# Turning the merged chunks by VectorE and GpSimd DMAs, and adding x by accumulating DMAs, in a hybrid attention and RG-LRU layer

## The reference, cut to what matters

```
g = sigmoid(h @ w_gate + b_gate)          # two halves, g_a and g_r
merged = g_a * (y_a @ w_br_attn) + g_r * (y_r @ w_br_rnn)
out = merged @ w_out                      # 4096 x 4096
y = x + gate_res * out                    # gate_res: one value per channel
```

## Time and profile before

| | |
|---|---|
| median of 3 runs | 2569.64 us (2569.23 to 2569.82) |
| the profiled execution's own time | 2569.65 us |
| its span, first to last instruction | 2567.8 us |
| TensorE busy | 2534.8 us, 99% |
| VectorE busy | 2010.9 us, 78% |
| ScalarE busy | 1441.0 us, 56% |
| GpSimd busy | 38.2 us, 1% |

### The profile page before, as it was taken

One profiled execution on the slowest core, in us unless ns is written; L12 is line 12 of the kernel. 1 busy time (PEld: TensorE's weight loads), 2 busy tenths in 40 slices (PEclk: granted clock), 3 DMA queues, 4 the chain that ended last, 5 costly groups with the idle time before them and its releaser, 6 DMA issues.

```text
span 2567.8 us, 31417 instructions
## 1 busy us (share of the span) xinstructions
PE 2534.8 (99%) x11463; PEld 2102.1 (82%) x11463; DVE 2010.9 (78%) x2138; ACT 1441.0 (56%) x1712; POOL 38.2 (1%) x58
## 2 busy tenths in 40 slices
PE   6999999999999999999999999999999999999999
PEld 5888888888888888888888888888888888878887
DVE  6999999999887666675766766668787878778885
ACT  6787766655554465655666666543434444544453
POOL 0000000000000000220000000000000000000000
PEclk9999999999999999999999999999999999999999
DMA  9999999999998566556666666689898989666674
GB/s 351 360 329 348 349 366 356 378 366 353 354 359 288 171 195 187 156 162 196 194 198 199 194 200 198 201 320 352 306 356 311 351 312 349 212 219 214 205 238 164
DMA packets 374846, 700.86 MB, mean 273 GB/s; under 512 B 28082, under 2 KB 83620, under 8 KB 374436
## 3 DMA queue, kind: packets, MB, share of 16 engines
q1 hardware_dynamic: 374176, 698.72, 80.9%
q10 hardware_dynamic: 516, 0.13, 0.0%
HBM read 694.55 MB, written 4.21 MB: 272 GB/s over the span
## 4 chain that ended last, share of the span: by engine, by line
PE 97%; DVE 1%; ACT 1%; SPq 0%; issue 0%; DMA 0%; DVEq 0%; ACTq 0%
PE ps_acc L1629 27%; PE ps_acc L1564 25%; PE ps_acc L1566 25%; PE ps_t L1564 3%; PE ps_t L1566 3%; PE ps_t L1629 3%; PE ps_acc L1580 2%; PE ps_acc L1582 2%; PE ps_acc L1621 0%; PE ps_acc L1622 0%; PE ps_acc L1623 0%; DVE w_lo L996 0%; PE ps_t L1704 0%; SPq L606 0%; DMA ada_first<-in_w_ada 0%
## 5 line engine op out<-in xcount | busy, mean ns | idle before, releaser
L741 ACT ACTIVATE w_hi<-land 128x1024 fp32r<-128x1024 f32 x860 | 910.3, 1060 | 948.3 <-PE ps_acc L1566 614.1
L996 DVE TENSOR_TENSOR w_lo<-land,w_hi 128x1024 fp32r<-128x1024 f32 x860 | 1049.2, 1222 | 416.1 <-ACT w_hi L741 412.9
L1564 PE MATMUL ps_acc<-w_hi,h_hi 128*128 128x512 f32 x2324 | 907.3, 390 | 0.1
L1566 PE MATMUL ps_acc<-w_hi,h_lo 128*128 128x512 f32 x2324 | 904.5, 389 | 0.0
L1629 PE MATMUL ps_acc<-w_lo,h_hi 128*128 128x512 f32 x2564 | 685.7, 389 | 0.6 <-DVE w_lo L996 0.6
L1629 PEld LDWEIGHTS ps_acc<-w_lo,h_hi 128*128 128x128 f32 x2564 | 481.1, 188 | 101.4 <-DVE w_lo L996 1.4
L1564 PEld LDWEIGHTS ps_acc<-w_hi,h_hi 128*128 128x128 f32 x2324 | 436.3, 188 | 91.1 <-ACT ps_acc L880 0.5
L1566 PEld LDWEIGHTS ps_acc<-w_hi,h_lo 128*128 128x128 f32 x2324 | 436.4, 188 | 89.4
L1005 DVE SCALAR_TENSOR_TENSOR acc<-ada_ring,cvec,acc 128x1024 f32<-128x1024 f32 (+1 forms) x291 | 300.1, 1031 | 15.0 <-DMA ada_ring<-in_w_ada 8.3
L1406 DVE SCALAR_TENSOR_TENSOR racc<-res_land,cvec,racc 128x1024 f32<-128x1024 f32 x124 | 158.5, 1279 | 0.8 <-DMA res_land<-in_w_ada 0.7
L1564 PE MATMUL ps_t<-w_hi,h_hi 128*128 128x512 f32 x356 | 138.7, 389 | 0.0
(11 more groups left out here) (307 smaller groups left out, 2192.0 us busy)
## 6 DMA issues: line engine op xcount, KB each, us to landing
land<-in_w_in SPq DMA_DIRECT2D x384, 512.0 KB, 5.5
land<-in_w_gate SPq DMA_DIRECT2D x256, 512.0 KB, 4.5
ada_ring<-in_w_ada SPq DMA_DIRECT2D x160, 512.0 KB, 6.1
res_land<-in_w_ada SPq DMA_DIRECT2D x128, 512.0 KB, 7.7
land<-in_w_out SPq DMA_DIRECT2D x92, 512.0 KB, 4.4
ada_ring<-in_w_ada SPq DMA_DIRECT2D x140, 256.0 KB, 5.0
land<-in_w_br_attn SPq DMA_DIRECT2D x64, 512.0 KB, 4.3
land<-in_w_br_rnn SPq DMA_DIRECT2D x64, 512.0 KB, 5.8
```

Source lines behind the costliest of these rows:

```text
L741: act.activation(w_hi[:, n % PARTS], land[:, n % LAND], ACT.Copy).then_inc(hi_rdy, 1)
L996: dve.tensor_tensor(w_lo[:, n % PARTS], land[:, n % LAND], w_hi[:, n % PARTS].bitcast(F32), ALU.subtract).then_inc(split_done, 1)
L1564: pe.matmul(sums[:, t], l_hi(kk, t), w_hi[:, n % PARTS, kk], start=first and kk == 0 and not added, stop=False, skip_group_check=added)
L1566: ins = pe.matmul(sums[:, t], l_lo(kk, t), w_hi[:, n % PARTS, kk], start=False, stop=False, skip_group_check=added)
```

## The change

Three parts go together.

1. *Turning.* After the merged add of chunk k, VectorE turns the chunk in blocks of 32 by 32 by two transposes of 128 by 512 into `gate_turned`, which has the place of `gate`. GpSimd then issues sixteen DMAs, each of 32 partitions by 1 KB (32 KB), that put the blocks in place in `chunk_t[k]`. SP's bias load of the next block waits for these sixteen (`mt_in`) where it waited for `gate_used`. ScalarE and VectorE read `chunk_t` where they read `ps_t`; TensorE's transposes and the copies into `comb` are gone.
2. *x.* At units 600 and 624 SP issues two copies of x into y, DRAM to DRAM, each of 128 rows by 3584 columns (1.84 MB). The results of the first seven chunks are added to y by accumulating DMAs on GpSimd's queue. The loads of x and stores of y in SP's program go, but for the last chunk's.
3. *Emptying.* ScalarE copies LEFT and RIGHT (and "out" 0) into the SBUF tile `plain`, on which TensorE now waits (`plain_kept`), and VectorE joins from `plain`.

The diff, without the declarations of semaphores and some removed lines:

```diff
+X_AT = [N_R + 24, N_R + 48]
...
-    if FREED[j][0] == "dve" or JOBS[j][:2] == ("out", 0):
+    if FREED[j][0] == "dve":
...
+def by_block(tiles):
+    return tiles.rearrange("p k t (i b) -> p (k t) i b", b=32)
+def by_tile(blocks):
+    return blocks.rearrange("p i k t b -> p (k t) i b")
...
-        x_out = at("x_out", [P, 2, NT, CW], F32, blk(88))
+        plain = at("plain", [P, 4, CW], F32, blk(88))
...
-        comb = [at(f"comb{i}", [P, UK, NT, P], F32, blk(32 + 4 * i)) for i in range(SEVENS)]
+        gate_turned = at("gate_turned", [P, BPJ, BPJ, NT, 32], F32, r_scr)
+        chunk_t = [at(f"chunk_t{k}", [P, BPJ, BPJ, NT, 32], F32, blk(V_BLK + 4 * k)) for k in range(CH)]
         tsum = at("tsum", [P, 4, CW], F32, blk(40))
+        x_last = at("x_last", [P, NT, CW], F32, blk(40))
...
+            for k in range(CH):
+                pool.wait_ge(chunk_turned, k + 1)
+                for i in range(BPJ):
+                    for jj in range(BPJ):
+                        pool.dma_start(chunk_t[k][32 * jj:32 * jj + 32, i].rearrange("p a t b -> p (a t b)"),
+                                       gate_turned[32 * i:32 * i + 32, jj].rearrange("p a t b -> p (a t b)")
+                                       ).then_inc(mt_in, 16)
+            pool.wait_ge(y_x, 16 * len(X_AT))
+            pool.wait_ge(out_rdy, 1)
+            pool.dma_start(y_v[:, :, 0:CW], plain[:, 2:4], accum_op=ALU.add).then_inc(added, 16)
+            for q in range(JOINT):
+                pool.wait_ge(out_rdy, q + 2)
+                for i in range(2):
+                    cc = 2 * q + 1 + i
+                    pool.dma_start(y_v[:, :, cc * CW:(cc + 1) * CW], whole[:, 2 * i:2 * i + 2], accum_op=ALU.add
+                                   ).then_inc(added, 16)
...
-                            sp_.wait_ge(gate_used, g - CH)
+                            sp_.wait_ge(mt_in, (g - CH) * 16 * BPJ * BPJ)
...
-                if n == N_O + 6:
-                    sp_.wait_ge(unit_done, N_O)
-                if n == N_O + 8:
-                    load_x(0, 0)
+                if n in X_AT:
+                    t = X_AT.index(n)
+                    sp_.dma_start(y_v[:, t, 0:(CH - 1) * CW], x_v[:, t, 0:(CH - 1) * CW]).then_inc(y_x, 16)
...
-                for q in range(JOINT):
-                    if n == JOINT_AT[q] + 8:
-                        sp_.wait_ge(out_rdy, q + 1)
-                        for cc in ((2 * q - 1, 2 * q) if q else (0,)):
-                            store_y(cc)
-                    if n == JOINT_AT[q] + 12:
-                        load_x(2 * q + 1, q)
-                        load_x(2 * q + 2, q + 1)
                 if n == N_END + 8:
-                    sp_.wait_ge(out_rdy, JOINT + 1)
-                    store_y(CH - 3)
-                    store_y(CH - 2)
-                if n == N_END + 12:
-                    load_x(CH - 1, JOINT)
+                    sp_.wait_ge(seven_lo, 3 * len(SEVEN_AT))
+                    sp_.dma_start(x_last[:], x_v[:, :, (CH - 1) * CW:]).then_inc(x_last_in, 16)
             for t in range(NT):
                 sp_.wait_ge(out_rdy, JOINT + 2 + t)
-                sp_.dma_start(y_v[:, t, (CH - 1) * CW:], x_out[:, slot_of(CH - 1), t]).then_inc(stored[slot_of(CH - 1)], 16)
-            sp_.wait_ge(stored[slot_of(CH - 2)], 16 * CH // 2)
-            sp_.wait_ge(stored[slot_of(CH - 1)], 16 * CH // 2 + 16)
+                sp_.dma_start(y_v[:, t, (CH - 1) * CW:], whole[:, t]).then_inc(stored, 16)
+            sp_.wait_ge(added, 16 * (CH - 1))
+            sp_.wait_ge(stored, 16 * NT)
...
             def mt_round(k):
-                act.wait_ge(mt_t, k + 1)
-                act.activation(h_hi[:, k * BPJ:(k + 1) * BPJ], mt_ps, ACT.Copy).then_inc(mt_h, 1)
+                act.wait_ge(unit_done, N_O - RU)
+                act.wait_ge(mt_in, (k + 1) * 16 * BPJ * BPJ)
+                act.activation(by_block(h_hi[:, k * BPJ:(k + 1) * BPJ]), by_tile(chunk_t[k][:]), ACT.Copy
+                               ).then_inc(mt_h, 1)
...
-            def keep_tiles(i):
-                act.wait_ge(mt_t, i + 1)
-                act.activation(comb[i][:], mt_ps[:, 0:UK], ACT.Copy).then_inc(comb_in, 1)
...
-                    act.wait_ge(out_rdy, q + 1)
+                    act.wait_ge(added, (2 * q + 1) * 16)
                 else:
                     act.wait_ge(comb_l, SEVENS)
                 act.activation(whole[:, 0], ps_c[:], ACT.Copy).then_inc(first_kept, 1)
+            def keep_chunk():
+                act.wait_ge(unit_done, N_O + GU)
+                act.activation(plain[:, 2:4], accs[RIGHT_ACC], ACT.Copy).then_inc(plain_kept, 1)
...
+            def keep_left(q):
+                act.wait_ge(unit_done, JOINT_AT[q] + 2 * len(EIGHT) - 1)
+                if q:
+                    act.wait_ge(joined, q)
+                act.activation(plain[:, 0:2], accs[LEFT_ACC], ACT.Copy).then_inc(plain_kept, 1)
+            def keep_right(q):
+                act.wait_ge(unit_done, JOINT_AT[q] + 2 * len(EIGHT))
+                if q:
+                    act.wait_ge(joined, q)
+                else:
+                    act.wait_ge(added, 16)
+                act.activation(plain[:, 2:4], accs[RIGHT_ACC], ACT.Copy).then_inc(plain_kept, 1)
...
+                if n == N_O + GU + 1:
+                    keep_chunk()
+                for q in range(JOINT):
+                    if n == JOINT_AT[q] + 2 * len(EIGHT):
+                        keep_left(q)
+                    if n == JOINT_AT[q] + 2 * len(EIGHT) + 1:
+                        keep_right(q)
...
-                    dve.tensor_tensor(merged[:, index], merged[:, index], gate[:], ALU.add).then_inc(gate_used, 1)
-                if kind == "out" and index == 0:
-                    dve.wait_ge(xo_in[slot_of(0)], 16)
-                    dve.wait_ge(rg_rdy, CH)
-                    st.did(dve.tensor_tensor(sums, sums, res_gate[:, 0].unsqueeze(1).to_broadcast([P, NT, CW]), ALU.mult))
+                    st.did(dve.tensor_tensor(merged[:, index], merged[:, index], gate[:], ALU.add))
                     st.sync()
-                    dve.tensor_tensor(x_out[:, slot_of(0)], sums, x_out[:, slot_of(0)], ALU.add).then_inc(out_rdy, 1)
+                    for t in range(NT):
+                        ins = dve.transpose(gate_turned[:, :, :, t], merged[:, index, t].rearrange(
+                            "p (k j a) -> p j k a", k=BPJ, j=BPJ))
+                        if t == 0:
+                            st.did(ins)
+                    ins.then_inc(chunk_turned, 1)
+            def gate_chunk():
+                dve.wait_ge(plain_kept, 1)
+                dve.wait_ge(rg_rdy, CH)
+                dve.tensor_tensor(plain[:, 2:4], plain[:, 2:4], res_gate[:, 0].unsqueeze(1).to_broadcast([P, NT, CW]),
+                                  ALU.mult).then_inc(out_rdy, 1)
...
-                dve.wait_ge(comb_in, i + 1)
-                (a11, a21), (a12, a22) = [[comb[i][:, kk, t] for t in range(NT)] for kk in range(UK)]
+                dve.wait_ge(mt_rdy, i + 1)
+                (a11, a21), (a12, a22) = [[chunk_t[i][:, :, kk, t] for t in range(NT)] for kk in range(UK)]
...
-            def join_left(q):
-                dve.wait_ge(unit_done, JOINT_AT[q] + 2 * len(EIGHT) - 1)
-                st.did(dve.tensor_tensor(whole[:, 0], accs[LEFT_ACC][:, 0], whole[:, 0], ALU.add))
-                dve.tensor_tensor(whole[:, 1], accs[LEFT_ACC][:, 1], whole[:, 1], ALU.subtract).then_inc(plain_free, 1)
-            def join_right(q):
-                dve.wait_ge(unit_done, JOINT_AT[q] + 2 * len(EIGHT))
+            def join_plain(q):
+                dve.wait_ge(plain_kept, 2 * q + 3)
                 dve.wait_ge(mixed_free, q + 1)
-                st.did(dve.tensor_tensor(whole[:, 2], accs[RIGHT_ACC][:, 0], whole[:, 2], ALU.add))
-                dve.tensor_tensor(whole[:, 3], accs[RIGHT_ACC][:, 1], whole[:, 3], ALU.add).then_inc(plain_free, 1)
+                st.did(dve.tensor_tensor(whole[:, 0], plain[:, 0], whole[:, 0], ALU.add))
+                st.did(dve.tensor_tensor(whole[:, 1], plain[:, 1], whole[:, 1], ALU.subtract))
+                dve.tensor_tensor(whole[:, 2:4], plain[:, 2:4], whole[:, 2:4], ALU.add).then_inc(joined, 1)
             def gate_whole(q):
                 sums = whole[:].rearrange("p (c t) n -> p c t n", c=2)
                 st.sync()
-                dve.wait_ge(plain_free, 2 * q + 2)
-                st.did(dve.tensor_tensor(sums, sums, res_gate[:, 2 * q + 1:2 * q + 3].unsqueeze(2)
-                                         .to_broadcast([P, 2, NT, CW]), ALU.mult))
-                st.sync()
-                for cc in (2 * q + 1, 2 * q + 2):
-                    dve.wait_ge(xo_in[slot_of(cc)], (cc // 2 + 1) * 16)
-                dve.tensor_tensor(x_out[:], sums, x_out[:], ALU.add).then_inc(out_rdy, 1)
+                dve.wait_ge(joined, q + 1)
+                dve.tensor_tensor(sums, sums, res_gate[:, 2 * q + 1:2 * q + 3].unsqueeze(2)
```

(71 more changed lines are left out.)

## The result

The changed kernel takes **2613.97 us** (median of 4 runs, 2612.14 to 2615.17) against 2569.72 us before (4 runs, 2569.23 to 2569.82) on the same chip: ratio 1.0172, 95% interval 1.0157 to 1.0187. It is slower, as forecast, by 44 us instead of 82. The profiled execution took 2612.14 us, its span is 2610.3 us.

A forecast was written before the change was run, and what follows sets the result against it. TensorE, busy 99% of the span, bounds the kernel. Stalls with their low clock 91.0 us, plus copies 6, less gains 14.4, give +82.6 on 2569.65: 2652 us; range 2585 to 2705 us.

The forecast's parts named there:

- rival A: GpSimd hands its DMAs over almost for free, flying side by side; no stall at block changes, 2561 us; chance 0.10.
- Rival B: The sixteen turning DMAs go one after another, each landing before the next, 54 us; some 2940 us; chance 0.05.
- Rival C: The adding DMAs into y end late, after the last joint stage; 20 us late at twice the price, 2672 us; chance 0.05.
- the price of an issue: GpSimd's cost to issue one turning DMA: taken as 1.0 us, between 0.43 and 1.28.
- the late landing: Load behind SP's wait lands as late as the one before did, 7.6 us: 22 us on top over seven changes.
- The stalls together: TensorE late at seven block changes behind SP's wait: four of 11.9 us, three of 10.5, sum 79.1 us.
- The clock behind them: Lower TensorE clock after each of the seven stalls: 1.7 us each, 11.9 us together.
- The copies: Copies of x into y ahead of the loads of units 601 and 625: 3 us each, 6 us.
- The transposes on VectorE: They delay `lo` of unit 602 by 1.4 us against 0.9 slack; 0.5 us vanishes, else 2 us without the stall.
- The gains: What TensorE gets back: transposes 7.4 us, waits of the joint stages 5.3, clock 1.7, sum 14.4 us.
- the joint stages: TensorE's five waits on VectorE's PSUM reading go, 5.3 us, plus 1.7 us of low clock after the longest.
- the turning: TensorE's transposes of the merged chunks go: 0.92 us a chunk, eight chunks, 7.4 us, all on the path.

The follow-up runs named there:

- experiment 1: Changed kernel with SP's bias load and its wait for the sixteen turning DMAs six units later from the second chunk on: 2560.18 us, ratio 0.9964.
- experiment 3: Changed kernel with each of the sixteen turning DMAs split into two of half the bytes, 32 issues a chunk: 2673.16 us, ratio 1.0404.
- experiment 7: Changed kernel with bias load and wait six units later, x copies at units 484 and 524, VectorE's transposes one unit later: 2554.59 us, ratio 0.9944.
- the version without the losses: Changed kernel with SP's bias wait six units later, x copies early and VectorE's transposes one unit later: 2554.59 us.
- experiment 5: Kernel before, TensorE still turning, with the changed kernel's joint stage and adding DMAs, and x copies at units 484 and 524: 2559.95 us, ratio 0.9964.
- the fastest version: Changed kernel with SP's bias wait six units later, x copies early and VectorE's transposes one unit later: 2554.59 us, ratio 0.9944.

## Why the prediction was right and where it was not

**Right:** the mechanism and its place. SP's in-order wait holds the load of the unit after; seven waits, at the changes that were named; the granted clock at 0.50 behind each; nothing left at the joint stages; no turning on TensorE. Moving the wait alone (experiment 1) takes 53.8 us off, the whole loss of 44 and more, and rival A's outcome, 2561 us, appears there, but by moving the wait and not by a free hand-over. Rival B's landings one after another did not come: a landing takes 2.1 us and the issues come every 0.50. Rival C did not come either: the last adding DMAs are issued by 2574.13 and land some 10.2 us later, 20 us ahead of the last matmuls; but a load of weights beside them landed after 11.89 us, and the eighth wait (0.95 us) stands behind it, which the text had not priced. The Trainium skill's fit (DMA: Bandwidth & Descriptors, Anatomy of one DMA) gives 2.08 us for 32 KB, and the median landing of 2.1 us agrees, as long as SP is held; beside SP's loads it is 3.9 or 4.7. For 16 KB the fit gives 2.04 us, and the median was 1.6 (experiment 3).

**Wrong in size: the price of an issue**, which the text named as the term that decides and took at 1.0 us. It is 0.50, near the lower end of 0.43. For the change after unit 648, term by term, forecast against trace:

- merged add to first issue: 1.45, measured 1904.05 - 1902.44 = 1.61;
- fifteen issues: 15.0, measured 7.32;
- landing of the last: 3.4, measured 2.12;
- the loads ahead in SP's queue: 1.4, measured 1914.84 - 1913.50 = 1.34;
- landing of the load behind the wait: 4.5, measured 8.20;
- rounding: 1.06 and 1.06.

26.8 us forecast, 21.7 measured (1902.44 to 1924.12 is the sum with the gaps between). The wait should then be 11.9 - 5.1 = 6.8 us; it is 5.95. TensorE's own delay of 0.34 us at 1906.12 (a `w_lo` that the transposes made late), some 0.6 with the slower matmuls around it, is most of the rest. So an error of 7.7 us in the issues and 1.3 in the landing was partly made good by one of 3.7 the other way: the load behind the hold. With the issue alone put right the sum would have been 2652 - 7 x 7.7 = 2598 us, too low by 16; that the misses partly cancel is luck. I took the median load and put the late landing into the range alone. The released SP sends its backlog in one go, the bias and eight 512 KB loads between 1913.50 and 1919.94, and the first to matter shares the engines with the rest.

**The stalls together:** 79.1 us forecast, 35.7 measured. **The clock behind them** was undersized: 11.9 forecast. From GpSimd's first issue of chunk 0 to that of chunk 7 the changed kernel takes 2272.77 - 1756.57 = 516.2 us, experiment 1 2220.39 - 1756.56 = 463.8; the 52.4 us between them less the 35.7 of waiting leave 16.7, or 2.4 a stall in place of 1.7. After the wait of 5.95 us thirteen matmul intervals (5.7 us) ran at the low clock, after the 2.77 us of the earlier trace rows nine.

**The copies:** 6 us forecast, 3.4 measured beside the transposes, and at most 1 without them. All of it is the first copy's: behind the second, at unit 624, TensorE shows no wait, where the text counted 3 us for each. **The transposes on VectorE:** the text said that the 0.5 us they make `w_lo` late vanish in the stall, and would be 2 us without it; without the stalls they are 2.1 us (experiment 7).

**The gains:** 14.4 us forecast, and 14.6 measured in the version without the losses. Within the sum two parts are off the other way round: the joint stages gave 9.3 us (experiment 5) in place of 7.0, the turning 14.6 - 9.3 = 5.3 in place of 7.4. The traces show most of both. The text gave the short waits of the joint stages no price beyond themselves: units 804 to 823 take 84.77 us before and 82.96 in experiment 5, 1.81 us for two waits of 1.00 and 0.23 at a granted clock of 1.00. And it said that there are five waits in the output part, where the kernel before has a sixth, in the last chunk, which also goes:

```profile
PE ps_acc L1629 <- DVE w_lo L996: 0.6, 1, 0.6
```

The turning itself was priced rightly: units 768 to 775, with four of the eight turnings, take 26.31 us before and 22.67 in the fastest version, 0.91 us for each. Some 0.8 us is lost again in the last wait behind the adding DMAs and some 1 us in delays of 0.1 to 0.3 us between units 603 and 758, whose cause was not tried.

Two smaller slips change nothing in the forecast. At 0.32 us an issue the seven stalls of rival A come to 7.7 us by the text's own sum, not 8.4. The two `wrg` loads are issued 0.51 us apart (1176.99 and 1177.50), not less than 0.5; they fly together all the same.

## What to carry to other kernels

Where a wait is moved to an in-order queue, ask first what stands behind it there: here it was not the DMAs but their wait's place in SP's order that cost 54 us. A hold of SP's queue of 7.2 us cost 7.5 us here, although the loads are early enough to forgive some of it, since the backlog that it releases lands late (8.2 us for 4.5) and a stalled TensorE comes back at the low clock (2.4 us a stall). A transfer that only just arrives in time should be waited for where the next user needs it, not where the next user's own load happened to be issued.

## What the runs showed of the hardware

- A GpSimd DMA of 32 partitions takes 0.50 us to issue, with 1 KB or 512 B a partition; the median landing, with SP held, went from 2.1 to 1.6 us.
- The landing of such a DMA depends on SP's traffic: 2.1 us with SP held, 3.9 and 4.7 with its loads running.
- The adding DMAs of 512 KB into y are another matter (issues of the page: count, KB each, median us to landing):

```profile
out_y<-in_x SPq DMA_DIRECT2D x2, 1792.0 KB, 10.3
...
out_y<-whole POOLq DMA_DIRECT2D x6, 512.0 KB, 10.2
```

  They land after 10.2 us, as late as a copy of x three and a half times their size, and a load of weights beside two of them took 11.8 us (experiment 7), where the median of `land` from `w_out` is 4.6.

- The clock fell after a TensorE wait of 2.17 us too (experiment 1; 0.50 in the stretch from 1760 to 1762 us), and not after a wait of 1.00 us (the kernel before; 1.00 in all stretches from 2350 to 2358) nor after waits of 0.33 us (1.00 in all stretches around them).
